# Attention and gate products of a hybrid block: two stages' matmuls laid into one, and the mixing steps in another order

## The reference

```
hn = rmsnorm(h, norm1_g)
u, q, k, v, g_ssm, g_att = split(hn @ w_in)        # g_ssm, g_att: 1024 columns each
y = gelu(s5(u));  y_ssm = y * sigmoid(y @ glu_w + glu_b)             # width 512
for each of 4 heads, query blocks of 128:
    s[j] = q[j] @ k[j].T - slope * distance, causal, j = 0, 1        # q, k of width 64
    w = softmax(s[0]) - lam * softmax(s[1])
    o = w @ v                                                        # v of width 128
y_att = rmsnorm(o, subln_g) * 0.8
mixed = sigmoid(g_ssm) * (y_ssm @ w_ssm_out) + sigmoid(g_att) * (y_att @ w_att_out)
h = h + mixed @ w_o
```

## Time and profile before

| | us |
|---|---|
| median of 3 runs | 2569.73 |
| the profiled execution | 2566.05 |
| its span, first to last instruction | 2564.3 |
| attention stage, 239.9 to 330.8 | 90.9 |
| mix stage, 330.8 to 560.8 | 230.0 |
| TensorE busy over the span | 2175.6 (85%) |
| VectorE busy | 1388.6 (54%) |
| ScalarE busy | 919.6 (36%) |
| mean granted TensorE clock | 0.851 |

### The profile page before, as it was taken

How to read it: one execution, slowest core, us unless ns; L and a number is a source line. 1 busy time by engine, 2 the same in 40 slices (tenths; PEclk the granted TensorE clock), 3 DMA queues, 4 the chain that set the end, 5 groups by cost and what they waited for, 6 DMA issues and landing times. The chain is left out here.

```text
span 2564.3 us, 29257 instructions
## 1 busy us (share of the span) xinstructions
PE 2175.6 (85%) x11628; PEld 1805.3 (70%) x11628; DVE 1388.6 (54%) x1959; ACT 919.6 (36%) x1342; POOL 111.3 (4%) x167
## 2 busy tenths in 40 slices
PE   2898889989999898999564999659979998559993
PEld 2897589978999786863353888547968777548882
DVE  4962632626554545312443999654136664459995
ACT  3452353221010005310222777431124561437772
POOL 0432000000000000000001000000000000010000
PEclk9987589989999998985585999879875799569997
DMA  5332022314222222210124999822430001069993
GB/s 154 93 86 50 0 68 98 118 42 105 92 84 83 82 83 79 91 50 0 35 69 156 350 397 401 295 75 72 117 84 1 1 1 66 19 216 385 395 396 132
DMA packets 170071, 328.42 MB, mean 128 GB/s; under 512 B 39809, under 2 KB 104481, under 8 KB 169809
## 3 DMA queue, kind: packets, MB, share of 16 engines
q1 hardware_dynamic: 126800, 281.47, 31.1%
q0 software_dynamic: 9520, 27.43, 3.4%
q10 hardware_dynamic: 33616, 17.65, 2.7%
HBM read 301.29 MB, written 19.99 MB: 125 GB/s over the span
## 5 line engine op out<-in xcount | busy, mean ns | idle before, releaser
L2013 PE MATMUL ps<-m_ws,m_xbT 128*128 128x512 f32 x1344 | 318.8, 394 | 2.8 <-DVE m_xbT L2178 2.8
L2013 PEld LDWEIGHTS ps<-m_ws,m_xbT 128*128 128x128 f32 x1344 | 255.4, 190 | 56.9 <-DVE m_xbT L2178 3.6
L2171 DVE TENSOR_TENSOR m_ws<-ring,m_ws 128x2048 fp32r<-128x2048 f32 x112 | 255.8, 2289 | 33.6 <-ACT m_ws L2063 31.5
L1493 PE MATMUL ps<-ffT,ff_ws 128*128 128x264 f32 (+1 forms) x1056 | 241.2, 323 | 4.7 <-DVE ff_ws L409 4.7
L2063 ACT CAST m_ws<-ring 128x2048 fp32r<-128x2048 f32 x112 | 213.3, 1910 | 77.9 <-PE ps L2013 48.3
L1493 PEld LDWEIGHTS ps<-ffT,ff_ws 128*128 128x128 f32 x1056 | 176.4, 190 | 20.4 <-DVE ff_ws L409 4.8
L1493 PE MATMUL ps<-ffT_lo,ff_ws 128*128 128x264 f32 (+1 forms) x528 | 170.1, 322 | 0.0
L2039 PE MATMUL ps<-m_ws,m_hT 128*128 128x512 f32 x672 | 166.8, 397 | 0.0
L1291 PE MATMUL ps<-hT,mx_ws 128*128 128x264 f32 x768 | 143.4, 287 | 7.3 <-DVE mx_ws L196 6.4
L2039 PEld LDWEIGHTS ps<-m_ws,m_hT 128*128 128x128 f32 x672 | 122.2, 188 | 23.1
L2168 DVE TENSOR_TENSOR m_ws<-ring,m_ws 128x2048 fp32r<-128x2048 f32 x56 | 128.2, 2290 | 8.6 <-ACT m_ws L2061 7.7
(11 more groups left out here) (463 smaller groups left out, 4182.2 us busy)
## 6 DMA issues: line engine op xcount, KB each, us to landing
ring<-in_moe_w_gate SPq DMA_DIRECT2D x112, 512.0 KB, 5.4
ring<-in_moe_w_up SPq DMA_DIRECT2D x112, 512.0 KB, 7.5
ring<-in_moe_w_down SPq DMA_DIRECT2D x56, 1024.0 KB, 8.3
ring<-in_w_up SPq DMA_DIRECT2D x22, 1024.0 KB, 5.1
ring<-in_w_in SPq DMA_DIRECT2D x16, 1024.0 KB, 6.5
ring<-in_gla_w_in SPq DMA_DIRECT2D x12, 1024.0 KB, 5.1
ring<-in_w_down SPq DMA_DIRECT2D x11, 1024.0 KB, 4.9
ring<-in_nsa_w_in SPq DMA_DIRECT2D x10, 1024.0 KB, 7.3
```

What stands on the lines that cost most here:

```text
L1493: ins = nc.tensor.matmul(ps[:, bank, 0:b - a], w[j][:, k, s * P:(s + 1) * P], x[l][:, k, a:b], start=(k == 0 and j == l), stop=(k == KD - ...
L2013: ins = nc.tensor.matmul(ps[:, it % 2, :], xbT[:, blk % 2, a, 4 * half + k, :].bitcast(F32R), v[b][:, k, :], start=(half == 0 and k == 0 a ...
L2171: ins = V.tensor_tensor(o, x.rearrange("p (j k w) -> p j k w", k=4, j=2), x0, ALU.subtract)
```

## The change

The attention stage becomes `attend_stage` and takes over the sixteen gate tiles. Its TensorE list runs 23 turns; 32 gate halves (24 passes each) are shared out over them, one or two a turn, and after each pass as many of the turn's attention instructions (a generator `attention(it)`) are laid in as keep both counts in step. Gates are copied raw to `gT` by ScalarE. PSUM: scores in banks 0 and 1, their columns over 512 in bank 4 with a small matmul and a small VectorE instruction each, transposes in 2 and 3, the product with v in bank 5 alone, gates in 6 and 7. VectorE's remainders of slabs 2 to 9 stand at the end of its turns. In the mix stage GLU comes first, then the means, then the products with w_ssm_out and with w_att_out; the weight order is changed to match. ScalarE takes four Ln, then four Exp, and puts the sigmoid on the raw gates in place.

```diff
+def mix_turns():
+    return [("u", i) for i in range(4)] + [("m", i) for i in range(H1)] + [(x, i) for x in "sa" for i in range(KD)]
...
+        self.n_so = self.fm_slabs(A["w_ssm_out"][0], 0, 2, 512)
         self.n_ao = self.fm_slabs(A["w_att_out"][0], 0, 2, 512)
-        self.n_so = self.fm_slabs(A["w_ssm_out"][0], 0, 2, 512)
...
+        turns = N + 3
+        halves = [range(32 * it // turns, 32 * (it + 1) // turns) for it in range(turns)]
+        turn_of = {hh: it for it in range(turns) for hh in halves[it]}
...
+                        for j in range(2):
+                            q, k = (qk[64 * j:64 * j + 64, 4 * x + hd] for x in range(2))
+                            ins = nc.tensor.matmul(ps[0:nq, j, 0:min(nk, 512)], q[:, q0:q0 + nq], k[:, 0:min(nk, 512)], start=True, stop=True)
...
+                            yield
...
-                        if u >= 2:
-                            pe.wait_ge(o_out, u - 1)
+                        if u:
+                            pe.wait_ge(o_out, u)
...
+                for it in range(turns):
+                    pieces, total, n_pass, n_step = attention(it), steps(it), 0, 0
+                    passes = 24 * len(halves[it])
+                    for hh in halves[it]:
+                        i, hf = divmod(hh, 2)
+                        a, e = HALVES[hf]
+                        wt = S.both(pe, i // 2, slab_view(KD, 256))
+                        if hh >= 2:
+                            pe.wait_ge(gate_out, hh - 1)
+                        for k in range(KD):
+                            for wa, xa in THREE:
+                                ins = nc.tensor.matmul(ps[:, 6 + hf, 0:HALF], ...)
...
+                                n_pass += 1
+                                while n_step * passes < total * n_pass:
+                                    next(pieces)
+                                    n_step += 1
...
ScalarE, at the end of each turn:
+                    for hh in halves[it]:
+                        i, hf = divmod(hh, 2)
+                        act.wait_ge(gate_done, hh + 1)
+                        nc.scalar.copy(gT[:, i, HALF * hf:HALF * hf + HALF], ps[:, 6 + hf, 0:HALF]).then_inc(gate_out, 1)
+                        if hh % 4 == 3:
+                            S.hi(act, hh // 4 + 2)
...
VectorE, scores, then at the end of each turn:
+                            if nk > 512:
+                                link(V.scalar_tensor_tensor(s[0:nq, it % 3, j, 512:nk], ...))
+                            n = min(nk, 512)
...
+                        V.tensor_copy(oT[:, hd, q0:q0 + nq], ps[:, 5, 0:nq]).then_inc(o_out, 1)
+                    for q in range(2, 10):
+                        if turn_of[4 * q - 5] == it:
+                            S.lo(dve, q)
...
mix stage, ScalarE:
+                for i in range(4):
+                    act.wait_ge(pr_done, at["u", i] + 1)
...
+                S.hi(act, 10)
+                for i in range(H1):
+                    act.wait_ge(pr_done, at["m", i] + 1)
+                    nc.scalar.activation(r[:, i].rearrange("p (a c) -> p a c", a=2), pair(at["m", i]), ACT.Ln, bias=eps[:]).then_inc(m_out, 1)
...
+                for i in range(8):
+                    nc.scalar.activation(gT[:, i], gT[:, i], ACT.Sigmoid).then_inc(gated, 1)
+                    if i == 3:
+                        S.hi(act, 11)
...
mix stage, VectorE: the s loop, lo(12), then the a loop with the sum and the remainders
+                for i in range(KD):
+                    c = at["s", i]
+                    dve.wait_ge(pr_done, c + 1)
+                    dve.wait_ge(gated, i + 1)
...
+                    V.tensor_tensor(g, g, pair(c).rearrange("p a (s n) -> p a s n", s=4), ALU.mult).then_inc(dve_out, 1)
+                    if i == 3:
+                        S.lo(dve, 11)
+                S.lo(dve, 12)
```

More of the change, by code:

```diff
@@ L1139, in _, with attention @@
             def _(pe):
-                for it in range(N + 3):
+                def attention(it):
                     if it < N:
@@ L1145, in _ @@
                             pe.wait_ge(s_read, it)
-                        for a in range(0, nk, 512):
-                            for j in range(2):
[L1148 to L1152, removed]
+                        for j in range(2):
+                            q, k = (qk[64 * j:64 * j + 64, 4 * x + hd] for x in range(2))
+                            ins = nc.tensor.matmul(ps[0:nq, j, 0:min(nk, 512)], q[:, q0:q0 + nq], k[:, 0:min(nk, 512)], start=True, stop=True)
+                            if j and nk <= 512:
+                                ins.then_inc(s_done, 1)
+                            yield
+                        if nk > 512:
+                            for j in range(2):
+                                q, k = (qk[64 * j:64 * j + 64, 4 * x + hd] for x in range(2))
+                                if j:
+                                    pe.wait_ge(m_done, hd + 1)
+                                ins = nc.tensor.matmul(ps[0:nq, 4, META * j:META * j + nk - 512], q[:, q0:q0 + nq], k[:, 512:nk], start=True, stop=True)
+                                ins.then_inc(s_done if j else m_done, 1)
+                                yield
                     u = it - 2
@@ L1176, in _, with steps @@
-                        ins.then_inc(o_done, 1)
+                            ins = nc.tensor.matmul(ps[:, 5, 0:nq], v[0:n, b, hd * P:(hd + 1) * P], wT[0:n, u % 2, b, 0:nq],
+                                                   start=(b == 0), stop=(b == i))
+                            if b == i:
+                                ins.then_inc(o_done, 1)
+                            yield
+                def steps(it):
+                    n = 0
+                    if it < N:
+                        n += 2 if shape[units[it][1]][1] <= 512 else 4
+                    return n + sum(units[u][1] + 1 for u in (it - 2, it - 3) if 0 <= u < N)
@@ new lines, in _ @@
+                for it in range(turns):
[9 more added lines that the diff above has]
+                            for wa, xa in THREE:
+                                ins = nc.tensor.matmul(ps[:, 6 + hf, 0:HALF], wt[wa][:, k, (i % 2) * P:(i % 2) * P + P],
+                                                       (hT, hlo)[xa][:, k, a:e].bitcast(F32R), start=(k == 0 and wa == xa),
+                                                       stop=(k == KD - 1 and wa == 1))
+                                if k == KD - 1 and wa == 1:
+                                    ins.then_inc(gate_done, 1)
+                                n_pass += 1
+                                while n_step * passes < total * n_pass:
+                                    next(pieces)
+                                    n_step += 1
+                    for _ in pieces:
+                        pass
@@ L1180, in _ @@
                 act.dma_start(alibi[:], self.const(1, "alibi")).then_inc(loaded, 16)
-                for it in range(N + 2):
+                S.hi(act, 0)
+                S.hi(act, 1)
+                for it in range(turns):
                     if it < N:
@@ L1212, in _ @@
                         for j in range(2):
[L1213 to L1215 removed]
+                            if nk > 512:
+                                link(V.scalar_tensor_tensor(s[0:nq, it % 3, j, 512:nk], alibi[0:nq, 400 - q0 + 512:400 - q0 + nk],
+                                                            2.0 ** (-2 * (hd + 1)), ps[0:nq, 4, META * j:META * j + nk - 512], ALU.mult, ALU.add))
+                            n = min(nk, 512)
+                            V.scalar_tensor_tensor(s[0:nq, it % 3, j, 0:n], alibi[0:nq, 400 - q0:400 - q0 + n], 2.0 ** (-2 * (hd + 1)),
+                                                   ps[0:nq, j, 0:n], ALU.mult, ALU.add).then_inc(s_read if j else own, 1)
                         link.n += 1
@@ L1296, in _ @@
                 for c, (what, i) in enumerate(turns):
[L1297 to L1304, removed]
+                    if 4 <= c < NA:
+                        pe.wait_ge(u_out if turns[c - 4][0] == "u" else m_out, turns[c - 4][1] + 1)
+                    elif NA <= c < NA + 4:
+                        pe.wait_ge(u_out if turns[c - 4][0] == "u" else m_out, turns[c - 4][1] + 1)
+                    elif c >= NA + 4:
+                        pe.wait_ge(dve_out, c - 3 - NA)
+                    if what == "m":
                         pe.wait_ge(sq_done, i + 1)
@@ L1336, in _ @@
                     act.dma_start(to, frm).then_inc(loaded, 16)
-                S.hi(act, 0)
-                S.hi(act, 1)
                 act.wait_ge(start, 1)
+                for i in range(4):
+                    nc.scalar.copy(yh[:, i].bitcast(F32R), yT[:, i]).then_inc(y_hi, 1)
                 for hd in range(H1):
                     nc.scalar.activation(sq[:, hd], oT[:, hd], ACT.Square).then_inc(sq_done, 1)
-                for i in range(4):
-                    nc.scalar.copy(yh[:, i].bitcast(F32R), yT[:, i]).then_inc(y_hi, 1)
```

(35 more changed lines are left out.)

100 lines of the change are left out of this document (41 added, 59 removed).

## The result

The changed kernel takes 2603.95 us (median of 4 runs, 2603.58 to 2610.79) against 2569.28 for the kernel before in the same session: ratio 1.0144, 95% interval 1.012 to 1.0167. It is slower by about 35 us; the forecast was slower by 7. The direction was right and the size was not, and the time lies outside the range of 2556 to 2598.

What follows compares the result with a forecast made beforehand. Attention was bound by a chain through TensorE, VectorE and ScalarE, later stretches by matmul passes. Attention 192.5 plus mix 135.8 gave 328.3 us against 320.9, 7.4 slower: 2577 us by the median, range 2556 to 2598.

Steps and rivals of the forecast that it cites:

- The place of the loss: Attention stage: TensorE's v product waits for bank 5 until VectorE's copy, last in its turn; the stage takes 192.5 us.
- Stalls, forecast 35: Attention stage: TensorE waits 35 us for VectorE's copy, longest in turns after a slab split; bounds 10 and 45.
- TensorE's work, forecast 142.6: Attention stage: gate passes 93.7, scores 23.5, transposes 7.0 and v products 18.4 us.
- start 4.7, cold start 2.2 and end 5.0: Attention stage: 4.7 us before the first pass, 2.2 for cold passes, 4.7 + 0.3 after the work.
- the price of a lone score matmul: Attention stage: separated score halves lose their overlap, which eats the clock's gain, so scores stay at 23.5 us.
- The clock, forecast 3 us: Attention stage: clock falls after long stalls cost 2.2 us each, 3 us taken in all.
- the prediction's own sign: Attention stage: a clock near 1.0 would show the forecast right, one under 0.9 wrong.
- Rival 3: Attention stage: the clock falls often, a fifth of the work at half rate; +20 us, 2597 us; chance 0.19.
- upper bound of 13 us: Attention stage: six stalls over 3 us, each with a clock fall of 2.2 us, make at most 13 us.
- The mix stage, forecast 135.8: Mix stage: start 4.5, GLU 13.9, wait 6.2, s and a 46.9, last product 5.1, end 59.2 us.
- 1 (TensorE alone sets the turns, 164.5 us): Attention stage: VectorE's chain never sets a turn; stage 164.5 us, kernel 2549 us; chance 0.18.
- 2 (pairs keep overlapping): Attention stage: score pairs overlap or weight loads hide behind gate passes; 11.8 us less work, 2569 us; chance 0.13.

Runs made afterwards that it cites:

- copy-first run: Changed kernel with VectorE's copy of the finished v product moved from the end to the head of its turn: 2559.76 us, ratio 0.9986 to the kernel before.
- both: Changed kernel with VectorE's v-product copy at the head of its turn and its remainders of slabs 2 to 9 one turn later: 2555.16 us, ratio 0.9967.
- with pairs: The kernel of "both" with the two score matmuls of j = 0 and j = 1 adjacent, no gate pass between: 2539.41 us, ratio 0.9909.
- run of filled waits: Changed kernel with 12 unused gate passes added on TensorE ahead of each of its 19 waits for VectorE's copy: 2599.02 us, ratio 1.0124.

## Why the prediction was right or wrong

**The place of the loss** was right: the attention stage, at the v product that waits for VectorE's last instruction of a turn. Both stages' rows and the copy-first run show it.

**Stalls, forecast 35, measured 20.4.** The turn lengths were worked out with too little TensorE work; with more, the copy comes earlier against the product. This reason is argued, not tested. The prediction's list of turns had the two causes about even (16.4 of its 33.5 us in turns behind a split); in the runs the place of the 0.3 us copy is the larger part (41 us against 7).

**TensorE's work, forecast 142.6.** This term was too small. The stage beside waits and clock is 173.3 us; less start 4.7, cold start 2.2 and end 5.0 it is 161.4, 19 more. The step that failed is the price of a lone score matmul: I had kept the paired time at half clock, which is as if only columns counted. The row of "both" shows 1.26 us for 0.85 of columns: 0.3 around the matmul itself and 0.11 in the step of the pass behind it. Read in the same way over all gate passes of that run, the 400-key unit costs 2.1 and the 272-key one 1.7, and all scores of the stage come to 38.0 us instead of 23.5. The products with v come to 21.0 instead of 18.4: the 40 with 128 rows cost 0.22 each, under the forecast 0.28, but the 20 with 16 rows some 0.6. The transposes take 7.9 instead of 7.0. These make 18.0 of the 19 us. The 0.4 us beyond the columns go with matmuls on 16 or 64 rows between passes on 128. What fills them no run separated; a weight load as such does not, since the 128-row fp32 matmul has its loads too and costs its columns only.

**The clock, forecast 3 us, measured 24.5.** This is the step that failed most, and the prediction's own sign of it is there: 0.83, under 0.9. I read two waits of the front stage, one of 2.50 us with no fall and one of 4.08 with one, as if a wait had to be near 4 us long. After the change falls follow waits of 2.94 and even 1.54 us. And I let the price be one cold start of 2.2 us, while a fall at the 512-column scores lengthened everything in that turn, and the next wait (1.55 us) came before the clock was up again: the stretch from 317.6 lasted 17.1 us. Rival 3 had this mechanism, at 0.19, and its +20 us is near the 21.5 that were missing. Its time of 2597 still stays 7 us short of the 2604 measured, since neither it nor the forecast had the larger work. The upper bound of 13 us for this term did not hold either, for the same reason.

**The mix stage, forecast 135.8, measured 139.4.** By its steps: start 5.0 for 4.5, GLU 14.0 for 13.9, wait 6.8 for 6.2, s and a 48.6 for 46.9, 5.2 for 5.1, end 59.8 for 59.2. The one term with a cause is 46.9: the wait ahead of it was 3.2, and behind it the clock fell. The sigmoids on the raw gates stayed hidden.

The sum: 18.8 of work, -14.6 of stalls, 21.5 of clock, 3.6 of mix stage make 29.3, and 7.4 + 29.3 = 36.7, the growth of the two stages. The stalls that were put too high hid part of what was put too low: with 20.4 in their place the same sum would have said 7.2 us faster. That the direction came out right was in part luck.

**Rivals.** 1 (TensorE alone sets the turns, 164.5 us) is what "both" became, at 173.9 with the work as it is, and at 159.0 with pairs. 2 (pairs keep overlapping) did not happen; it was worth 15 us, not 12. The rule of the Trainium skill weighed there (TensorE: Matmul & The Clock Gate, "Part 3: Packing small matmuls") holds in this case: 0.73 us for four records adjacent, 0.72 for two alone. The warning of the same page under "A second HAM failure mode: psum-queue depth-cycling" holds too: waits of 1.5 to 3.2 us between groups brought the clock down six times.

## What to carry to other kernels

When work is laid into a stream of matmuls, follow each result bank back to the instruction that frees it and ask where in its engine's list that instruction stands: one copy at the end of a turn instead of its head cost 41 us here, more than half of it through the clock. Price a TensorE wait in a mixed stream above its length: 20.4 us of waits cost 24.5 more through the clock here, and 28.0 us of waits only 12.6 more where the score pairs were adjacent. Do not take a tolerated wait elsewhere as a licence. Keep matmuls on different halves of the rows adjacent.

## What the runs showed of the hardware

- The granted clock fell at a wait of 2.94 us in a stretch with 64-row and transposing matmuls, and behind 1.54 us where lone 512-column 64-row scores followed; a wait of 2.50 us in the front stage's dense passes did not lower it, nor did one of 1.6 in the run of filled waits. A wait of 1.8 us for ScalarE's copy was followed by a fall in the copy-first run (at 398.4) and by none in "both". The same scores with no wait around them ran at 1.00. So here the length of a wait alone did not tell whether the clock fell.
- A lone 64-row fp32 matmul of 512 columns among 128-row passes cost 1.26 us at the higher clock, of which 0.85 are columns, and a pair on both halves of the rows no more than that. Of 128 columns, one with 16 rows cost 0.62, one with 128 rows 0.22, less than the 0.28 it had as half of its cold time in a row.
- With 27.8 us of added passes whose results nobody reads, the stage's clock was 0.98 instead of 0.83 and the kernel's time no longer than without them.
